# Routed experts of a mixture-of-experts layer: a flat loop over pairs of row blocks, two buffers per stage of a block, and lookup tables in block order

## The chip, the core and the metric

The kernel runs on one core of one Trainium2 chip. The metric is the device time of one execution in microseconds (us), lower is better. TensorE is called PE in the profile, VectorE DVE, ScalarE ACT, GpSimd POOL and SyncE SP; PEld is the part of PE that loads the stationary operand.

## What is computed

One decoder layer over 1024 tokens of width 1024, in float32: a token mixer (gated delta rule and a convolution branch), a normalisation, a mixture of experts with 64 experts, and a normalisation. The change touches the experts:

```python
eidx, wts = route(xf, w_router, router_bias)      # 8 of 64 experts for each of 1024 tokens
# the 8192 (token, expert) pairs, sorted by expert, in blocks of 128 rows; each block has one expert
def expert_block(args):
    xblk, e = args
    hid = jax.nn.silu(xblk @ w_gate[e]) * (xblk @ w_up[e])     # 1024 -> 256
    return hid @ w_down[e]                                     # 256 -> 1024
y = segment_sum(yb * row_w[:, None], row_tok)                  # weighted sum over a token's 8 rows
```

An expert's weights are 3 MB (gate and up 1 MB each, down 1 MB), 192 MB for all 64. A block whose expert has fewer rows is padded.

## The kernel before

Every fp32 matmul operand is split in two fp32r parts (`hi`, rounded by ACT, and `lo`, the rest, by DVE), and a product is three matmuls (`split3`, lines 58 to 60). The stage `experts` (from line 1983) works expert by expert; an expert owns one to eight blocks. Which engine does what:

- SP loads the weights in six pieces of 512 KB an expert into six raw buffers `e_raw`, each when DVE has finished with that buffer (L2050 to L2058).
- ACT rounds a piece (`e_hi`, `ed_hi`, L2193), DVE subtracts (`e_lo`, `ed_lo`, L2250). The pieces of expert e+2 are split during the first block of expert e; there are three sets of split weights.
- POOL gathers a block's 128 token rows by an indirect DMA into a landing buffer `x_landing` (L2076), copies them to `x_gather` (L2084) once PE has transposed the rows before, and scatters the finished rows `y_block` four blocks later (L2096, `LAG` = 4). Landing buffer, `x_gather`, `gu_ps`, `hidden` and `y_block` exist once.
- PE does for a block: 24 matmuls gate|up, with the 8 transposes of the next block's rows after the 18th (L2130); 12 matmuls `down` of the previous block; 2 transposes of this block's `hidden` (L2153), which wait for ACT's silu (L2207) and DVE's product (L2260).
- ACT and DVE handle, in program order, the split pieces 0 to 3, the activation, the split of the next block's rows (`xg_hi` L2196, `xg_lo` L2255), the copy of y (L2201, before the split of `hid` on ACT), the split of `hid` (L2214, L2265), then pieces 4 and 5.

The loop over experts is unrolled by three (`all_experts`, L2038), so that PE's operand addresses are constants. For each expert every engine loads two numbers from the table `plan` into registers, the number of its blocks and the number of its first one (L2030, L2031), and loops over the blocks.

The stage before it, `block_tables` (L1948), turns the 64 x 8 x 128 slots of the routing (expert, block, row) into three tables with one column for each of the 512 possible blocks: token, weight and output row. Here 64 experts have 93 blocks. In this text a "single" is an expert with one block.

Of the kernel before, what the change touches and what calls it, by code (L numbers as in the profile page):

```python
# [16 lines left out]
F32 = mybir.dt.float32  # L17
# [29 lines left out]
MAXB = S * TOPK // P + E  # L47

# [20 lines left out]
class Kernel:  # L69
# [50 lines left out]
    def constants(self):  # L120
# [21 lines left out]
        self.credit_d = nc.dram_tensor("credit", (2, P, 1), F32, kind="Internal").ap()  # L142
# [19 lines left out]
    def load_x(self):  # L162
        nc, a = self.nc, self.a
        with ExitStack() as ctx:
# [59 lines left out]
            def _(pool):  # L224
# [15 lines left out]
                link(g.memset(junk[:], NONE))  # L240
                g.memset(junk[:, :, 1:2], 0.0).then_inc(fill_ready, 2)
# [1399 lines left out]
    def shared_and_route(self):  # L1641
# [3 lines left out]
        with ExitStack() as ctx:  # L1645
# [34 lines left out]
            nb = sb(ctx, "n_blocks", [P, E])  # L1680
            nbc = sb(ctx, "n_blocks_cum", [P, E])
# [123 lines left out]
            def _(dve):  # L1805
# [102 lines left out]
                step(v.tensor_copy(self.plan[:, :, 0:1], nb[0:1, :].unsqueeze(2)))  # L1908
                step(v.tensor_copy(self.plan[:, :, 1:2], nbc[0:1, :].unsqueeze(2)))
# [10 lines left out]
            def _(pool):  # L1920
# [27 lines left out]
    def block_tables(self):  # L1948
# [3 lines left out]
        with ExitStack() as ctx:  # L1952
            rows = sb(ctx, "slot_rows", [P, Q, P, 3])
            ps = ctx.enter_context(nc.psum_tensor("tab_ps", [P, 3, Q, P], F32))
            r_in, tr_done, tab = self.sems(ctx, "rows_in", "tab_tr", "tab_done")
            cols = [sb(ctx, f"tab_col{i}", [P, Q, P]) for i in range(3)]
            block = ctx.enter_context(nc.Block())
# [17 lines left out]
            def _(pe):
                for i in range(3):
                    pe.wait_ge(tab, i + 1)
                    for q in range(Q):
                        last = nc.tensor.transpose(ps[:, i, q, :], cols[i][:, q, :], self.ident[:])
                    last.then_inc(tr_done, 1)  # L1980


    def experts(self):

        nc, sb, a = self.nc, self.sb, self.a
        with ExitStack() as ctx:
            PIECES = 6
            BUFS = 3
            SLOTS = 6
            LAG = 4  # L1990
            raw = [sb(ctx, f"e_raw{q}", [P, 4 * FF]) for q in range(SLOTS)]
            wh = [sb(ctx, f"e_hi{j}", [P, KT, 2, FF], F32R) for j in range(BUFS)]
            wl = [sb(ctx, f"e_lo{j}", [P, KT, 2, FF], F32R) for j in range(BUFS)]
            dh = [sb(ctx, f"ed_hi{j}", [P, 2, D], F32R) for j in range(BUFS)]
            dl = [sb(ctx, f"ed_lo{j}", [P, 2, D], F32R) for j in range(BUFS)]
            xl_d = sb(ctx, "x_landing", [P, D])
            xg = sb(ctx, "x_gather", [P, D])
            xh = sb(ctx, "xg_hi", [P, KT, P], F32R)
            xl = sb(ctx, "xg_lo", [P, KT, P], F32R)
            sg = sb(ctx, "gate_act", [P, FF])  # L2000
            hid = sb(ctx, "hidden", [P, FF])
            hh = sb(ctx, "hid_hi", [P, 2, P], F32R)
            hl = sb(ctx, "hid_lo", [P, 2, P], F32R)
            yb = sb(ctx, "y_block", [P, D])

            idx_g, idx_s = (sb(ctx, n, [P, 1], U32) for n in ("idx_gather", "idx_scatter"))
# [453 lines left out]
```

## Time and profile before

| | us |
|---|---|
| median of 3 timed runs (2982.14 to 2989.01) | 2988.53 |
| the profiled execution, its own time | 2998.25 |
| its span, first to last instruction | 2996.7 |
| PE busy (86%) | 2573.5 |
| DVE busy (62%) | 1864.5 |
| ACT busy (42%) | 1264.2 |
| POOL busy (26%) | 766.6 |

Times below are us from the start of the span. The expert stage starts at 1835.7 us with the first load of weights and ends at about 2865 us with the last scatter. Matmuls overlap in the profile: one of 512 columns is drawn as 0.39 us long while the next starts 0.23 us after it. PE's idle time and the distance between starts therefore say more than its busy sum. The granted clock (PEclk) is a share of full speed.

### The profile page before, as it was taken

What the parts mean: (1) busy time and instruction counts of PE and PEld (TensorE: products, weight loads), DVE (VectorE), ACT (ScalarE), POOL (GpSimd) and SP (SyncE); (2) the same over time, 40 slices, a digit from 0 to 9 for tenths busy, and PEclk for the clock granted to TensorE, in tenths of its full rate; (3) what the DMA queues carried; (4) which work ended last, traced back from release to release, by engine and by line L of the source; (5) the groups of instructions that cost most, each with busy time, mean ns of one, the idle gap of its engine ahead of it and who ended that gap; (6) DMA issues with size and microseconds to landing.
All of it is one profiled execution on the core that took longest, in us unless ns stands there. A gap on an engine that the chain in (4) does not pass through costs nothing. (4 is left out here: it accounts for less than half of the span.)

```text
span 2996.7 us, 39317 instructions
## 1 busy us (share of the span) xinstructions
PE 2573.5 (86%) x12548; PEld 2072.5 (69%) x12549; DVE 1864.5 (62%) x2441; ACT 1264.2 (42%) x1673; POOL 766.6 (26%) x888
## 2 busy tenths in 40 slices
PE   7989998998999999969977832899999989998956
PEld 5768777777877777747856721677777767776832
DVE  3346887787788655527446613676677676667428
ACT  3343453354345333335221102566566675566400
POOL 2012111222211111100002072444444444444300
PEclk9999999999999999989989965999999999999978
DMA  5423345342322353263543135788778787879367
GB/s 117 67 44 63 64 47 53 64 57 50 78 54 47 71 78 78 61 207 123 170 149 105 60 72 171 249 282 274 256 279 284 268 304 261 263 262 331 129 268 320
DMA packets 246349, 462.96 MB, mean 154 GB/s; under 512 B 26649, under 2 KB 151065, under 8 KB 244191
## 3 DMA queue, kind: packets, MB, share of 16 engines
q1 hardware_dynamic: 211870, 377.44, 45.1%
q0 software_dynamic: 34368, 84.04, 8.0%
q8 instruction: 72, 1.18, 0.2%
q14 instruction: 39, 0.31, 0.0%
HBM read 399.97 MB, written 93.87 MB: 165 GB/s over the span
## 5 line engine op out<-in xcount | busy, mean ns | idle before, releaser
L58 PE MATMUL dn_pj<-x_hi,dn_hi 128*128 128x512 f32 x1024 | 437.7, 427 | 5.1 <-DVE dn_lo L924 2.9
L60 PE MATMUL dn_pj<-x_hi,dn_lo 128*128 128x512 f32 x1024 | 411.0, 401 | 0.0
L59 PE MATMUL dn_pj<-x_lo,dn_hi 128*128 128x512 f32 x1024 | 409.8, 400 | 0.0
L1008 DVE SCALAR_TENSOR_TENSOR uc_half<-u_in,par,uc_half 128x512 f32<-128x512 f32 x480 | 383.3, 798 | 13.1
L2250 DVE TENSOR_TENSOR e_lo<-e_raw,e_hi 128x1024 fp32r<-128x1024 f32 x256 | 340.4, 1389 | 74.1 <-ACT e_hi L2193 68.0
L58 PE MATMUL gu_ps<-e_hi,xg_hi 128*128 128x512 f32 x744 | 317.8, 427 | 56.2 <-DVE xg_lo L2255 32.0
L2193 ACT ACTIVATE e_hi<-e_raw 128x1024 fp32r<-128x1024 f32 x256 | 251.9, 1052 | 141.6 <-DMA e_raw<-in_w_gate_e_dram 116.5
L60 PE MATMUL gu_ps<-e_hi,xg_lo 128*128 128x512 f32 x744 | 300.2, 403 | 0.0
L59 PE MATMUL gu_ps<-e_lo,xg_hi 128*128 128x512 f32 x744 | 300.0, 403 | 0.0
L1147 POOL TENSOR_TENSOR a_lvl<-a_t,lvl_mask 128x512 f32<-128x512 f32 x112 | 167.7, 1514 | 349.0 <-PE dn_a L686 221.1
L60 PEld LDWEIGHTS dn_pj<-x_hi,dn_lo 128*128 128x128 f32 x1024 | 198.5, 194 | 45.8
L58 PEld LDWEIGHTS dn_pj<-x_hi,dn_hi 128*128 128x128 f32 x1024 | 200.8, 196 | 39.3 <-DVE dn_lo L924 3.3
L59 PEld LDWEIGHTS dn_pj<-x_lo,dn_hi 128*128 128x128 f32 x1024 | 199.9, 195 | 34.7 <-issue 1.0
L58 PEld LDWEIGHTS gu_ps<-e_hi,xg_hi 128*128 128x128 f32 x744 | 145.6, 196 | 98.8 <-issue 68.0
L2084 POOL COPY x_gather<-x_landing 128x1024 f32<-128x1024 f32 x93 | 130.8, 1407 | 255.2 <-PE xg_ps L2130 191.7
L869 ACT ACTIVATE y_sb<-dn_a 128x256 f32<-128x256 f32 x96 | 36.8, 383 | 345.9 <-PE dn_a L686 345.5
L2250 DVE TENSOR_TENSOR ed_lo<-e_raw,ed_hi 128x1024 fp32r<-128x1024 f32 x128 | 153.4, 1239 | 31.9 <-ACT ed_hi L2193 24.2
L60 PEld LDWEIGHTS gu_ps<-e_hi,xg_lo 128*128 128x128 f32 x744 | 145.1, 195 | 33.2
L59 PEld LDWEIGHTS gu_ps<-e_lo,xg_hi 128*128 128x128 f32 x744 | 145.7, 196 | 25.3
L2201 ACT ACTIVATE y_block<-y_ps 128x1024 f32<-128x1024 f32 x93 | 95.3, 1025 | 150.4 <-PE y_ps L60 116.8
L58 PE MATMUL y_ps<-ed_hi,hid_hi 128*128 128x512 f32 x372 | 145.0, 390 | 2.4 <-DVE hid_lo L2265 2.4
L924 DVE TENSOR_TENSOR dn_lo<-dn_raw,dn_hi 128x1024 fp32r<-128x1024 f32 x62 | 92.8, 1498 | 86.6 <-ACT dn_hi L758 85.6
(346 smaller groups left out, 5183.1 us busy)
## 6 DMA issues: line engine op xcount, KB each, us to landing
e_raw<-in_w_gate_e_dram SPq DMA_DIRECT2D x128, 512.0 KB
e_raw<-in_w_up_e_dram SPq DMA_DIRECT2D x128, 512.0 KB
e_raw<-in_w_down_e_dram SPq DMA_DIRECT2D x128, 512.0 KB
dn_raw<-in_w_in_dram SPq DMA_DIRECT2D x64, 512.0 KB
y_rows<-y_rows SPq DMA_DIRECT2D x8, 2560.0 KB, 30.7
y_rows<-y_rows SPq DMA_DIRECT2D x8, 1536.0 KB, 25.1
gate_rows<-qkv_next SPq DMA_DIRECT2D x16, 512.0 KB, 3.1
br_raw<-in_w_oa_dram SPq DMA_DIRECT2D x16, 512.0 KB
```

Source lines behind the costliest of these rows:

```text
L58: nc.tensor.matmul(out, w_hi, x_hi, start=first, stop=False)
L59: nc.tensor.matmul(out, w_hi, x_lo, start=False, stop=False)
L60: return nc.tensor.matmul(out, w_lo, x_hi, start=False, stop=last)
L869: A(yy[:], ga[:, :, 0:P // 2], ACT.Copy).then_inc(y_evac, 1)
L924: tt(r["lo"][j][:], r["raw"][j][:], r["hi"][j][:].bitcast(F32), ALU.subtract).then_inc(r["w_ready"], 1)
L1008: ins = stt(out=uc[:], in0=u_in[:, t:t + HALF], scalar=w, in1=uc[:], op0=ALU.mult, op1=ALU.add)
L1147: tt(atl[l % NA][:], at[:], self.lvl_mask[:, l, :].unsqueeze(1).to_broadcast([P, 4, P]), ALU.mult).then_inc(masked, 1)
L2084: g.tensor_copy(xg[:], xl_d[:]).then_inc(x_here, 1)
L2193: A(h, r, ACT.Copy).then_inc(hi_s, 1)
L2201: A(yb[:], fl(yp[:]), ACT.Copy).then_inc(y_ready, 1)
L2250: tt(l, r, h.bitcast(F32), ALU.subtract).then_inc(lo_s, 1)
```

## The change

1. PE and POOL no longer loop over experts but over pairs of blocks (blocks 0 and 1, 2 and 3, ...), so that the buffer of a block is known by its parity. The number of blocks is rounded up to an even one, by a block without rows of the last expert. PE reads each block's expert from a table; its weight operands get their address from registers. ACT and DVE keep their loop over experts.
2. `x_gather`, `gu_ps`, `ht_ps`, `hidden` and its splits, and `y_block` have two buffers; the landing buffer and its copy are gone, the gather writes `x_gather` directly. The gather of a block is issued once PE has transposed the rows two blocks before it.
3. PE's order within a block is new: the 8 transposes of the next block come first, then 12 gate|up matmuls, the 2 transposes of the previous block's `hidden`, 12 gate|up matmuls, and the previous block's 12 `down` matmuls.
4. ACT and DVE take the split of the next block's rows and of `hid` first, and the weights in three pieces of 1 MB (two of gate|up, one of down) in three raw buffers. Gate|up are split two experts ahead, down in the first block of its own expert; split down weights have two sets.
5. `block_tables` makes tables in block order, of 128 columns: DVE works out which block each slot column belongs to, builds a 0/1 matrix `sel` and PE multiplies by it, where before it transposed.

```diff
-            raw = [sb(ctx, f"e_raw{q}", [P, 4 * FF]) for q in range(SLOTS)]
+            raw = [sb(ctx, f"e_raw{i}", [P, 2, 4 * FF]) for i in range(GU + 1)]
-                    pool.wait_ge(xg_in, n * 16 + 16)
-                    pool.wait_ge(t_done, n * 2 + 2)
-                    g.tensor_copy(xg[:], xl_d[:]).then_inc(x_here, 1)
+                    pool.wait_ge(idx_c, n + 1)
+                    pool.wait_ge(t_done, n * 2 + 2)
+                    pool.indirect_dma_start(xg[s][:], None, self.x1_d, bass.IndirectOffsetOnAxis(idx_g[s][:, 0:1], 0),
+                                            bounds_check=S - 1, oob_is_err=False).then_inc(xg_in[s], 16)
...
+                def blk(n, m, s, e, e_prev):
+                    pe.wait_ge(xl_s, n * 2 + 2)
+                    pe.wait_ge(xg_in[1 - s], (m + s) * 16 + 32)
+                    transposes(1 - s)
+                    pe.wait_ge(lo_s, e * GU + 1)
+                    gate_up(e, s, range(0, 4))
+                    if e_prev is not None:
+                        pe.wait_ge(hid_s, n)
+                        hid_t(1 - s)
+                    pe.wait_ge(lo_s, e * GU + 2)
+                    gate_up(e, s, range(4, 8)).then_inc(gu_done, 1)
+                    if e_prev is not None:
+                        pe.wait_ge(hl_s, n)
+                        pe.wait_ge(dlo_s, e_prev + 1)
+                        pe.wait_ge(y_ready, n + LAG - 1)
+                        down(e_prev, 1 - s)
...
+                with pe.Fori(1, half) as m:
+                    e_prev, e = expert_of(m * 2 - 1), expert_of(m * 2)
+                    e_next = expert_of(m * 2 + 1)
+                    blk(m * 2, m, 0, e, e_prev)
+                    blk(m * 2 + 1, m, 1, e_next, e)
...
+                    x_lo(n + 1, 0)
+                    x_lo(n + 1, 1)
+                    if not first or not known or e > 0:
+                        hid_lo(n - 1)
+                    if first:
+                        lo(e, GU)
+                    product(n)
+                    if ahead:
+                        lo(e + 2, 0)
+                        lo(e + 2, 1)
```

PE's program at the change of an expert, before: the transposes of `hidden`, then the loads of two numbers for the next expert (`TENSOR_LOAD plan`) with their register work, then the first gate|up matmul.

```order
L2153 MATMUL ht_ps<-ident,hidden 128x128
L2176 REGISTER_ALU
L2176 COMPARE_AND_BRANCH
L2175 UNCONDITIONAL_BRANCH
L2038 UNCONDITIONAL_BRANCH
L2038 ISA
L2030 TENSOR_LOAD plan
L2030 ISA x2
L2031 ISA
L2031 TENSOR_LOAD plan
L2031 ISA x2
L58 MATMUL gu_ps<-e_hi,xg_hi 128x512
```

The same engine now, at the start of the loop over pairs: three numbers are loaded for two blocks, behind the last `down` matmul of the pair before, and each group of three matmuls has two register instructions.

```order
L2257 TENSOR_LOAD block_expert
L2257 ISA x3
L2257 TENSOR_LOAD block_expert
L2257 ISA x2
L2232 MATMUL xg_ps<-ident,x_gather 128x128 x7
L59 MATMUL gu_ps<-e_hi,xg_hi 128x512
L60 REGISTER_ALU
L60 MATMUL gu_ps<-e_lo,xg_hi 128x512
L61 MATMUL gu_ps<-e_hi,xg_lo 128x512
L59 ISA
```

So the loads have left the place behind `hidden`, and register work has come between the matmuls. DVE's program in the first block of an expert, before (`hidden` stands behind four `e_lo`):

```order
L2250 TENSOR_TENSOR e_lo<-e_raw,e_hi 128x4x256
L2259 REGISTER_ALU
L2260 SCALAR_TENSOR_TENSOR hidden<-gate_act,wt_tab,gu_ps 128x256
L2253 ISA
L2255 TENSOR_TENSOR xg_lo<-xg_ps,xg_hi 128x512
L2265 TENSOR_TENSOR hid_lo<-ht_ps,hid_hi 128x256
```

and now:

```order
L2372 TENSOR_TENSOR xg_lo<-xg_ps,xg_hi 128x512
L2376 ISA
L2376 TENSOR_TENSOR hid_lo<-ht_ps,hid_hi 128x256
L2366 TENSOR_TENSOR ed_lo<-e_raw,ed_hi 128x2048
L2381 ISA x2
L2381 SCALAR_TENSOR_TENSOR hidden<-hidden,wt_tab,gu_ps 128x256
L2363 TENSOR_TENSOR e_lo<-e_raw,e_hi 128x2x4x256
```

`hidden` now stands ahead of both gate|up pieces and behind one down piece, and the next block's rows stand first.

## Rows read from the trace of the kernel before

**Rows 1.** Windows: start:end, length, busy us per engine (instructions), PEclk, DMA share, GB/s.
```profile
1825.50:1835.70 10.20, 2.82 (x12) 2.42 (x12) 3.40 (x6) 0.00 (x0) 0.00 (x0) 0.59 0.26 79
1835.70:1859.70 24.00, 1.97 (x8) 1.57 (x8) 7.97 (x8) 7.58 (x9) 9.81 (x14) 0.53 0.89 271
1859.70:1913.30 53.60, 40.44 (x172) 31.96 (x172) 36.18 (x38) 30.20 (x40) 24.76 (x31) 0.85 0.66 229
1913.30:2800.40 887.10, 816.71 (x3819) 662.51 (x3818) 616.60 (x681) 554.82 (x762) 375.78 (x496) 0.98 0.81 275
2410.20:2482.70 72.50, 62.27 (x276) 49.76 (x276) 57.55 (x60) 49.36 (x66) 27.44 (x36) 0.93 0.92 326
2494.00:2542.40 48.40, 47.59 (x230) 39.15 (x230) 28.79 (x35) 25.91 (x39) 19.78 (x30) 1.00 0.73 246
2900.00:2950.00 50.00, 39.85 (x74) 16.66 (x75) 34.55 (x40) 1.18 (x4) 0.00 (x0) 0.83 1.01 425
```

**Rows 2.** Timeline of PE: start, length, first gate|up matmul of five blocks, idle before.
```profile
2322.70 0.49 PE L58 MATMUL gu_ps<-e_hi,xg_hi 128*128 128x512 f32 x1
2332.06 0.50 PE L58 MATMUL gu_ps<-e_hi,xg_hi 128*128 128x512 f32 x1
...
2410.23 0.49 PE L58 MATMUL gu_ps<-e_hi,xg_hi 128*128 128x512 f32 x1 [1.18 <-DVE xg_lo L2255]
...
2482.72 0.49 PE L58 MATMUL gu_ps<-e_hi,xg_hi 128*128 128x512 f32 x1 [0.16 <-issue]
...
2553.58 0.49 PE L58 MATMUL gu_ps<-e_hi,xg_hi 128*128 128x512 f32 x1 [1.54 <-issue]
```

**Rows 3.** Waits, 1880 to 2840 us: who waited for whom, total, times, longest.
```profile
POOL x_gather L2084 <- PE xg_ps L2130: 191.7, 66, 8.3
...
ACT y_block L2201 <- DMA y_rows<-y_block,idx_scatter: 32.2, 12, 7.6
...
PE gu_ps L58 <- DVE xg_lo L2255: 30.5, 27, 1.6
...
PE gu_ps L58 <- issue: 22.8, 28, 2.0
PE ht_ps L2153 <- DVE hidden L2260: 22.5, 22, 6.3
...
ACT e_hi L2193 <- DMA e_raw<-in_w_up_e_dram: 6.9, 7, 2.2
```

**Rows 4.** PE and its sequencer at a change of expert: timeline, then the loads (ns min/median/max).
```profile
2302.36 0.49 PE L58 MATMUL gu_ps<-e_hi,xg_hi 128*128 128x512 f32 x1 [0.81 <-issue]
...
L2030 PEldq TENSOR_LOAD <-plan x65: 297/306/672, 1856.4 to 2855.6; - x65
```

**Rows 5.** Groups by line, 1800 to 2900 us: xcount | busy us, mean ns | idle before.
```profile
L2250 DVE TENSOR_TENSOR e_lo<-e_raw,e_hi 128x1024 fp32r<-128x1024 f32 x256 | 340.4, 1389 | 74.1 <-ACT e_hi L2193 68.0 <-issue 6.0
...
L2250 DVE TENSOR_TENSOR ed_lo<-e_raw,ed_hi 128x1024 fp32r<-128x1024 f32 x128 | 153.4, 1239 | 31.9 <-ACT ed_hi L2193 24.2 <-issue 7.7
...
L2084 POOL COPY x_gather<-x_landing 128x1024 f32<-128x1024 f32 x93 | 130.8, 1407 | 255.2 <-PE xg_ps L2130 191.7 <-DMA x_landing<-x_table,idx_gather 63.5
...
L2255 DVE TENSOR_TENSOR xg_lo<-xg_ps,xg_hi 128x512 fp32r<-128x512 f32 x188 | 120.2, 680 | 3.7 <-ACT xg_hi L2196 3.7
...
L2260 DVE SCALAR_TENSOR_TENSOR hidden<-gate_act,wt_tab,gu_ps 128x256 f32<-128x256 f32 x93 | 44.1, 474 | 111.3 <-ACT gate_act L2207 106.9 <-issue 4.4
L2265 DVE TENSOR_TENSOR hid_lo<-ht_ps,hid_hi 128x256 fp32r<-128x256 f32 x93 | 39.3, 422 | 118.8 <-ACT hid_hi L2214 111.9 <-issue 6.4
```

**Rows 6.** Timeline of the tables and of the start of the experts.
```profile
1832.78 0.69 DVE L1972 COPY wt_tab<-tab_ps 128x512 f32<-128x512 f32 x1 [0.16 <-PE tab_ps L1979]
...
1849.21 0.18 POOL L2092 COPY idx_scatter<-late_rows 128x1 uint32 x1 [6.19 <-DMA credit<-ong]
...
1855.27 1.03 POOL L2084 COPY x_gather<-x_landing 128x1024 f32<-128x1024 f32 x1 [2.89 <-DMA x_landing<-x_table,idx_gather]
...
1874.22 0.69 PE L2153 MATMUL ht_ps<-ident,hidden 128*128 128x128 f32 x2 [5.54 <-DVE hidden L2260]
```

More of the change, by code:

```diff
@@ L47 @@
 MAXB = S * TOPK // P + E
+LAG = 4
 COL_QKVZ, COL_AB, COL_GLU, COL_GA = 0, 4 * D, 4 * D + 2 * H, 6 * D + 2 * H
@@ new lines, in _ @@
+                tt(before[:], twice[:], ends[:, E - 1:E].to_broadcast([P, E]), ALU.is_lt)
+                step(v.tensor_scalar(gone[:], ends[:], part_no[:], None, ALU.is_le))
+                v.tensor_reduce(half[:], before[:], AX.X, ALU.add)
+                step(v.tensor_reduce(e_col[:], gone[:], AX.X, ALU.add))
+                v.tensor_scalar(e_col[:], e_col[:], float(E - 1), None, ALU.min).then_inc(tab, 1)
+                step(v.scalar_tensor_tensor(out=odd[:], in0=half[:], scalar=2.0, in1=base[:, E - 1:E], op0=ALU.mult,
+                                            op1=ALU.subtract))
@@ L1986, in experts @@
         with ExitStack() as ctx:
-            PIECES = 6
+            GU = 2
             BUFS = 3
-            SLOTS = 6
-            LAG = 4
-            raw = [sb(ctx, f"e_raw{q}", [P, 4 * FF]) for q in range(SLOTS)]
[L1992 to L2006, printed above, removed]
@@ L2007, in experts @@
-            late_rows = sb(ctx, "late_rows", [P, MAXB + NT + LAG], U32)
-            gu = ctx.enter_context(nc.psum_tensor("gu_ps", [P, 2, FF], F32))
+            raw = [sb(ctx, f"e_raw{i}", [P, 2, 4 * FF]) for i in range(GU + 1)]
+            wh = sb(ctx, "e_hi", [P, BUFS, KT, 2, FF], F32R)
+            wl = sb(ctx, "e_lo", [P, BUFS, KT, 2, FF], F32R)
+            dh = sb(ctx, "ed_hi", [P, 2, 2, D], F32R)
+            dl = sb(ctx, "ed_lo", [P, 2, 2, D], F32R)
+            xg = [sb(ctx, f"x_gather{s}", [P, D]) for s in range(2)]
@@ new lines, in experts @@
+            xh = sb(ctx, "xg_hi", [P, 2, KT, P], F32R)
+            xl = sb(ctx, "xg_lo", [P, 2, KT, P], F32R)
+            hid = sb(ctx, "hidden", [P, 2, FF])
+            hh = sb(ctx, "hid_hi", [P, 2, 2, P], F32R)
+            hl = sb(ctx, "hid_lo", [P, 2, 2, P], F32R)
+            yb = sb(ctx, "y_block", [P, 2, D])
+            idx_g = [sb(ctx, f"idx_gather{s}", [P, 1], U32) for s in range(2)]
+            idx_s = [sb(ctx, f"idx_scatter{s}", [P, 1], U32) for s in range(2)]
+            gu = ctx.enter_context(nc.psum_tensor("gu_ps", [P, 2, 2, FF], F32))
@@ L2114, in _ @@
-                total = pool.value_load(self.plan[0:1, E - 1, 1:2], min_val=0, max_val=MAXB - 1) + \
-                    pool.value_load(self.plan[0:1, E - 1, 0:1], min_val=1, max_val=NT)
+                half = pairs(pool)
+                with pool.Fori(0, half) as m:
+                    for s in range(2):
+                        n = m * 2 + s
+                        gather_rows(n, m, s)
+                        scatter_rows(n, s)
+                        gather(n, s)
+                        scatter(n, s)
@@ L2241, in _ @@
+                for i in range(GU):
+                    hi(0, i)
+                x_hi(0, 0)
+                x_hi(0, 1)
+                for i in range(GU):
+                    hi(1, i)
+                all_experts(act, blk)
+                total = pairs(act) * 2
+                hid_hi(total - 1)
+                y_move(total - 1)
             @block.vector
@@ L2282, in _ @@
+                for i in range(GU):
+                    lo(0, i)
                 x_lo(0, 0)
                 x_lo(0, 1)
-                for i in range(PIECES):
-                    lo(1, 1, i)
-                all_experts(dve, expert)
+                for i in range(GU):
+                    lo(1, i)
+                all_experts(dve, blk)
+                total = pairs(dve) * 2
+                hid_lo(total - 1)
     def final_norm(self):
```

447 lines of the change are left out of this document (252 added, 195 removed).

## The prediction

> **What bounds the kernel now.** I read the windows first, then block starts on PE, waits, and groups. The change lives in the expert stage, so everything before 1825.5 us and after the last scatter stays. From 1913.3 to 2800.4 us PE does 83 of the 93 blocks in 887.1 us, 10.7 us each, and DMA is busy 0.81 at 275 GB/s [rows 1]. A block in which PE waits for nothing takes 9.36 us (2322.70 to 2332.06) [rows 2]. So PE sets the pace, with 1.3 us a block lost. Where? The starts of the 83 blocks (the timeline's first is 1913.3, its last 2800.4) fall into kinds: 10 first blocks of a longer expert that follow a longer one take 9.4 us on average, 25 second or later blocks 9.9, 14 first blocks of a longer expert behind a single 10.5, 14 singles behind a longer expert 11.4 (one of them: 2542.4 to 2553.58, [rows 2]), and 20 singles behind a single 11.9. The stretch 2410.23 to 2482.72 is six such singles at 12.1 each [rows 2]; its DMA share is 0.92 at 326 GB/s. The stretch 2494.0 to 2542.4 is five blocks at 9.7, with 0.73 at 246 GB/s [rows 1].
>
> Two things hold a single back. First, order: DVE does four `e_lo` before `hidden`, then the rows of the next block, and PE waits at `ht_ps` for `hidden` (22.5 us in all), and at `gu_ps` for `xg_lo` (30.5) and for its own sequencer (22.8) [rows 3]. The last is the two table loads of a new expert, 0.3 us each plus register work; they stand behind the transposes of `hidden`, so when those have waited nothing hides them: gaps of 0.81 and 1.54 us [rows 2, 4]. ACT waits for weights hardly at all (6.9 us for the largest) [rows 3], so DMA is near its limit in runs of singles but not the one that ends last. Second, that limit: 326 GB/s over 72.5 us and six blocks is 3.94 MB a single; at share 1 the same traffic would run at 326/0.92 = 354 GB/s, 11.1 us a single. That is what a faster PE runs into.
>
> The Trainium skill bears on this: "HBM Reference" (Specifications) gives about 358 GB/s as the effective share of a core. By that figure alone a single would take 3.94/358 = 11.0 us, and the run of singles could gain no more than 1 us a block; it speaks against a large gain. The same page (Specifications) says that a core streaming alone reaches about 425 GB/s. This trace shows 425 in the last stage, from 2900 us, but in other traffic [rows 1].
>
> **The change, part by part.**
>
> *The waits at hidden, xg_lo and the copy.* PE's wait for `hidden` now stands behind down (12 x 0.23 = 2.7 us), 8 transposes and 12 gate|up matmuls, over 6 us after the gate|up sums it comes from; before it was 2.7 us. The next block's rows are transposed at the start of a block and needed one block later. DVE puts `hidden` ahead of the gate|up pieces. So 30.5 + 22.5 us go, where DVE keeps up. Its work for a single is now 4 x 1.22 (`e_lo`) + 2 x 1.24 (`ed_lo`) + 2 x 0.68 + 0.47 + 0.42 = 9.6 us [rows 5], 9.4 if large pieces save a little; I take 1.22 for `e_lo`, as its twin `ed_lo` has, since its mean of 1.39 comes beside POOL's copy (1.4 us x 93), which is gone. That is as long as PE's 9.36, so in a run of singles DVE is late, too, but by less than DMA. The Trainium skill, "GPSIMD Engine Reference" (Key points), says that GpSimd shares its SBUF interfaces with VectorE for instructions with two SBUF inputs, which `e_lo` is. By that, all of the 0.17 us x 256 = 44 us of DVE time is given back; it lies off PE's path except in runs of singles.
>
> *The copy and the landing buffer.* POOL waited 191.7 us for PE there [rows 3], which cost nothing: PE never waited for `x_gather` in steady state. Removed at 0. The new gather of a block is issued two blocks ahead of its use, some 19 us, so it is covered; without cover a landing would show as 3 to 12 us in front of the transposes.
>
> *Second y_block.* ACT waited 32.2 us for scatters, up to 7.6 at once [rows 3]; that falls to 0, and counts at the start below.
>
> *Sequencer.* Three loads for two blocks. One load is 0.31 us [rows 4]; where two stood uncovered the gap was 1.54 us [rows 2], so a load with its register work is about 0.77 us, and three with the loop's own steps are 2.6 us a pair. They stand behind the 12 `down` matmuls, whose wait (`hid_lo`) is met early, so 2.7 us of queued matmuls cover them. Bounds: 0 and 2.6 us a pair; I take 0.3, 0.15 us a block, near the lower end, because the wait ahead of the cover is early. The 24 register instructions that address the weights in a block are unlike anything PE did: the nearest are those around the loads: (1.54 - 2 x 0.31) us for the eight `ISA` of the order before, 0.12 us each. Two take 0.24 of the 0.68 us that three matmuls last, so I take 0; if they don't fit, rival C.
>
> Together: 9.36 + 0.15 = 9.5 us for 63 blocks (all but singles behind singles) = 598.5 us. An isolated single is late by at most 2 us in DMA and DVE, and the new slack of several us takes it.
>
> *Runs of singles, 20 blocks.* Bounds: 11.1 (DMA at share 1) and 12.5 (now 12.1 in the long run, plus 0.4 for coarser pieces: three 1 MB buffers wait for two 2.4 us steps each before they are refilled, where six smaller ones refilled sooner). Middle of 11.1 and 12.1: 11.6, so 232 us. After each of the 7 runs DVE and DMA catch up: 1.5 us each, 10.5 us (bounds 0 and 3). Sum 841 against 887.1: **-46 us**.
>
> *The start.* The gather of block 0 now waits for the credit DMA, which landed at 1849.21; before it went out as soon as the stage had begun (1835.7), its rows were copied at 1855.27 [rows 6], and the first gate|up came at 1859.7, 4.4 us behind. Now the issue comes after 1849.2, 13.5 us into the stage, and the second gather must land, too, before PE starts. If the landing takes as little as 3 us (an estimate: no row shows it alone), PE starts earlier than before; if it takes what was left of 19.6 us, 10 us later. I take 5 us later (bounds -1 and 10). Blocks 0 to 3 took 53.6 us [rows 1] with waits of 5.54 [rows 6] and 6.3 us [rows 3] for `hidden`, behind pieces and a late scatter; I take 9 back of these 11.8. Together **-4**.
>
> *An extra block.* 93 is odd, so PE does 94: **+9.4** (it moves no rows, but PE runs it whole).
>
> *The tables.* The stage took 10.2 us [rows 1], of which DVE waited for rows. New are some 21 small DVE operations, at 0.2 us for small ones and up to 0.69 us for 512 elements [rows 6], 7 us in all, of which 5 lie in the wait for the rows, less 1.4 us for narrower copies out of PSUM, and PE's products as the transposes before: **+3** (bounds 0 and 8).
>
> Sum: -46 - 4 + 9.4 + 3 = -37.6 us. The profiled execution of 2998.25 us is 9.7 above the median of 2988.53; I carry the difference over: 2951 us.
>
> **The rivals.**
>
> A (0.55), the forecast: runs of singles stay at DMA's limit, the rest goes at PE's pace.
>
> B (0.15), DMA isn't the limit. Share 0.92 in the run is queueing, and the 425 GB/s of [rows 1] can be had: 3.94 MB take 9.3 us. Then the 20 blocks take 9.6 and the catching up goes: -40 - 10.5 more, about 2900 us. For it: ACT hardly waits for DMA now. Against: 326 GB/s is the most that any stretch of weights and rows shows. The page on HBM named above holds both figures, and doesn't decide.
>
> C (0.18), slower: register instructions between the matmuls. PE's sequencer has two more per three matmuls. The point from which it decides: if a group's dispatch takes longer than 0.68 us. Each 0.1 us over costs 12 x 94 x 0.1 = 113 us, so 2951 + 113 = 3064 us; 0.04 us over is enough to be slower than before. For it: table loads do show as gaps at PE. Against: 0.24 us of 0.68, by the steps at the loads.
>
> D (0.12), no change that can be told (within 0.3%, 9 us, which is about what a measurement of this kernel can tell). Three raw buffers of 1 MB refill too late: a load waits for the end of a 2.1 us and a 2.4 us step of its own buffer, down is only one expert ahead, and each single, isolated or not, takes 12.1. Then 34 blocks take 12.1 = 411, 49 take 9.5 = 466: 877, and -10 - 4 + 9.4 + 3 = -2: 2987 us. For it: less is loaded ahead (7 MB instead of 9). Against: in one expert's time all three buffers still have a load in flight nearly always.
>
> **How the numbers follow.** Faster: A + B = 0.70. Same: D = 0.12. Slower: C = 0.18. The range goes from B's 2900, of which I leave some out, to beyond D: 2903 to 2996. A alone reaches from 20 x 0.5 + 10.5 lower (DMA at share 1, nothing to catch up) to 20 x 0.9 + 10.5 + 5 higher (12.5 us, catching up 3 us, a late start): 2931 to 2985.
>
> **What would show it.** In the trace after: PE's waits for `hidden` and `xg_lo` below 5 us together; blocks of longer experts at 9.4 to 9.6 us; in runs of singles 11.1 to 12.1 us, with a DMA share over 0.95 and ACT or DVE now waiting for `e_raw`; 94 blocks; gaps at the start of each pair below 0.5 us; `e_lo` at 2.4 us for 2048 elements; the first gate|up 42 us after the tables' stage began, against 34.2 before (1825.5 to 1859.7). If matmuls within a block start over 0.23 us apart, C is right; if the runs go at 9.5, B. The prediction fails, too, if the sequencer's loads aren't hidden behind down: 2.3 us more in each of 47 pairs is 108 us, and the gain is gone.

## The result, and the profile after

The changed kernel takes 3002.36 us (median; 2996.38 to 3007.55), the kernel before 2988.77 us in the same series: a ratio of 1.0044, 95% interval 1.0029 to 1.006. It is slower by about 14 us, 0.4%. The forecast was 2951 us, 1.3% faster, with a range of 2903 to 2996: wrong in sign, and outside the range.

The profiled execution took 3002.1 us, with a span of 3000.5. First the windows of the changed kernel, cut at the same events as [rows 1]: tables, start of the experts, blocks 0 to 3, blocks 4 to 86, a run of six one-block experts, and a stretch of longer experts.

```profile
1814.00:1826.90 12.90, 5.25 (x25) 4.79 (x25) 7.31 (x29) 0.00 (x0) 2.10 (x11) 0.58 0.21 62
1826.90:1856.80 29.90, 3.62 (x17) 3.22 (x17) 6.56 (x5) 7.44 (x6) 14.03 (x18) 0.52 0.66 195
1856.80:1899.80 43.00, 38.75 (x173) 31.23 (x171) 26.90 (x24) 24.24 (x26) 13.72 (x16) 0.90 0.70 249
1899.80:2793.80 894.00, 813.46 (x3820) 659.72 (x3820) 562.61 (x508) 541.68 (x590) 272.81 (x332) 0.97 0.78 272
2411.00:2485.20 74.20, 61.37 (x278) 48.52 (x278) 54.44 (x44) 48.78 (x48) 21.17 (x24) 0.95 0.91 323
2495.30:2543.00 47.70, 47.40 (x233) 38.92 (x232) 27.15 (x28) 29.55 (x35) 14.87 (x20) 1.00 0.63 221
```

Against [rows 1]: from the tables' first load to PE's first gate|up 42.8 us, before 34.2 (+8.6). Blocks 0 to 3 43.0, before 53.6 (-10.6). The 83 blocks 894.0, before 887.1 (+6.9, where the prediction had -46). From block 87 to the last stage's first transfer 84.4, before 74.7 (+9.7, the extra block). The last stage is longer by 0.7. That is +15.3 us. In the profile of before the stages ahead of the tables ended 11.6 us later than here (1825.7 against 1814.1); the change doesn't touch them. In all later profiles, one of a variant of the kernel before among them, this mark stands at 1808 to 1818, so it moves from one execution to another, and I leave it out. The medians differ by 13.6 us, near the sum of 15.3.

PE's stretch of longer experts runs as forecast: five blocks in 47.7 us, 9.54 each. The run of six one-block experts takes 74.2 us, before 72.5 [rows 1]. The waits of the changed kernel, 1880 to 2840 us, say who is late:

```profile
POOL y_rows L2200 <- ACT y_block L2322: 488.0, 69, 13.7
...
ACT e_hi L2303 <- DMA e_raw<-in_w_up_e_dram: 124.6, 70, 4.2
...
PE y_ps L59 <- DVE hid_lo L2376: 63.6, 30, 4.5
...
ACT y_block L2322 <- DMA y_rows<-y_block,idx_scatter: 38.3, 11, 6.4
...
PE xg_ps L2232 <- issue: 17.5, 23, 1.0
```

PE's waits for `xg_lo` (30.5 us in [rows 3]) and for `hidden` (22.5) are gone. In their place stands one at the down product, 63.6 us, for `hid_lo`. And ACT, which waited 6.9 us for weights [rows 3], now waits 124.6. The timeline of the changed kernel shows how the second makes the first (start, length, engine, operation, idle before and releaser):

```profile
2704.59 1.92 ACT L2303 ACTIVATE e_hi<-e_raw 128x2048 f32 x1 [2.48 <-DMA e_raw<-in_w_up_e_dram]
...
2705.32 0.33 SPq L2153 DMA_DIRECT2D e_raw<-in_w_gate_e_dram  x1
...
2706.68 2.29 DVE L2363 TENSOR_TENSOR e_lo<-e_raw,e_hi 128x2048 f32 x1 [1.52 <-ACT e_hi L2303]
...
2709.09 1.29 DVE L2372 TENSOR_TENSOR xg_lo<-xg_ps,xg_hi 128x512 f32 x2
2709.13 0.33 SPq L2153 DMA_DIRECT2D e_raw<-in_w_gate_e_dram  x1
2709.56 0.38 SPq L2153 DMA_DIRECT2D e_raw<-in_w_up_e_dram  x1
...
2710.29 0.41 DVE L2376 TENSOR_TENSOR hid_lo<-ht_ps,hid_hi  x1
...
2711.13 0.79 PE L59 MATMUL y_ps<-ed_hi,hid_hi 128*128 x1 [4.50 <-DVE hid_lo L2376]
...
2715.77 1.91 ACT L2303 ACTIVATE e_hi<-e_raw 128x2048 f32 x1 [2.90 <-DMA e_raw<-in_w_up_e_dram]
...
2717.59 1.01 ACT L2322 ACTIVATE y_block<-y_ps 128x1024 f32 x1
...
2717.85 2.29 DVE L2363 TENSOR_TENSOR e_lo<-e_raw,e_hi 128x2048 f32 x1 [1.94 <-ACT e_hi L2303]
...
2718.50 1.08 ACT L2309 ACTIVATE xg_hi<-xg_ps 128x512 f32 x2
...
2720.30 0.33 SPq L2153 DMA_DIRECT2D e_raw<-in_w_gate_e_dram  x1
```

Follow one raw buffer. DVE's low part ends at 2708.97; at 2709.13 SP asks for the next 1 MB into it (two transfers of 512 KB); at 2715.77 ACT can take it (6.6 us, in which ACT stood idle 2.90); ACT 1.91, DVE 2.29; at 2720.30 SP may ask again. This turn of the loop is 11.2 us long, and no step of it waited for PE.

How PE gets to wait is seen one turn earlier. ACT stood idle 2.48 us for the same buffer and began its `e_hi` at 2704.59; so DVE's `e_lo` began 1.52 us late, at 2706.68. ACT and DVE work in order: on ACT `y_block`, the next rows' `xg_hi` and `hid_hi` stand behind the `e_hi` that waited, on DVE `xg_lo` and then `hid_lo` (2710.29) behind the `e_lo`. PE comes to down after 12 matmuls and finds `hid_lo` 4.50 us late. The wait costs twice. The windows behind it (columns as above) show the granted clock at the lower level, 1.2 GHz, for most of the 12 matmuls of down (nine take 0.63 us instead of 0.39), and at 2.4 GHz again in the next block:

```profile
2711.10:2715.60 4.50, 4.47 (x11) 3.55 (x12) 4.26 (x3) 1.77 (x2) 2.80 (x1) 0.50 0.93 307
2716.90:2722.60 5.70, 5.70 (x28) 4.69 (x28) 3.91 (x4) 4.49 (x6) 2.26 (x4) 1.00 0.91 339
```

For the comparison of kernels I cut blocks 4 to 86 at each first gate|up matmul, and sort the 83 stretches by whether DVE splits a new expert's weights in them (between two activations). 25 are without weights; the others stand alone, or first, in the middle (20) or last in a row of such stretches. The expectations below call the 20 "singles behind singles" and the last ones "first blocks behind a single". In the kernel before the block named is the one whose gate|up opens the stretch; in the changed kernel, whose activations come later, the one before it. Means in us, worked out from the timelines; each row is one profiled execution, so a few us in the last column tell nothing:

| kernel | no weights | alone | first | middle | last | blocks 4 to 86 |
|---|---|---|---|---|---|---|
| before | 9.92 | 9.42 | 11.38 | 11.92 | 10.52 | 887.1 |
| after | 9.48 | 9.90 | 9.87 | 12.51 | 11.97 | 894.0 |
| e1_fine | 9.48 | 10.04 | 10.06 | 10.83 | 10.90 | 848.3 |
| e2_light | 9.48 | 9.90 | 9.87 | 10.50 | 10.47 | 831.1 |
| e3_early_hid | 9.31 | 9.32 | 10.55 | 12.08 | 11.07 | 872.2 |
| e4_before_coarse | 10.36 | 9.53 | 11.51 | 12.76 | 10.93 | 923.5 |
| e5_fine_early | 9.36 | 9.31 | 9.47 | 10.71 | 10.66 | 824.6 |
| e6_finer | 9.49 | 10.69 | 10.71 | 11.03 | 10.53 | 861.8 |
| e7_fine_copy | 9.50 | 10.33 | 10.16 | 11.35 | 10.89 | 862.9 |
| e8_fine_early_light | 9.31 | 9.33 | 9.42 | 9.41 | 9.54 | 779.9 |

### The profile page after: what moved, and what is told of

It is laid out like the page before. It is cut to its first block and busy times, and to the rows that moved or that the text cites. A ratio compares the mean times of both kernels' runs of the same rounds, so it can differ in the third digit from the quotient of the medians.

```text
span 3000.5 us, 42077 instructions
## 1 busy us (share of the span) xinstructions
PE 2580.1 (86%) x12607; PEld 2079.5 (69%) x12608; DVE 1809.9 (60%) x2274; ACT 1250.2 (42%) x1486; POOL 657.2 (22%) x718
## 5 line engine op out<-in xcount | busy, mean ns | idle before, releaser
L2303 ACT ACTIVATE e_hi<-e_raw 128x2048 f32 (+1 forms) x128 | 244.7, 1913 | 244.2 <-DMA e_raw<-in_w_up_e_dram 244.2
L2363 DVE TENSOR_TENSOR e_lo<-e_raw,e_hi 128x2048 f32 (+1 forms) x128 | 290.4, 2287 | 51.5 <-ACT e_hi L2303 51.2
L59 PE MATMUL gu_ps<-e_hi,xg_hi 128*128 (+1 forms) x752 | 310.4, 413 | 0.0
L2200 POOL DMA_INDIRECT y_rows<-y_block,idx_scatter x98 | 160.5, 1637 | 626.0 <-ACT y_block L2322 514.0
L61 PE MATMUL gu_ps<-e_hi,xg_lo 128*128 (+1 forms) x752 | 294.3, 391 | 0.0
L60 PE MATMUL gu_ps<-e_lo,xg_hi 128*128 (+1 forms) x752 | 293.5, 390 | 0.0
L2372 DVE TENSOR_TENSOR xg_lo<-xg_ps,xg_hi 128x512 f32 (+1 forms) x190 | 122.1, 684 | 168.4 <-ACT xg_hi L2309 154.9
L59 PE MATMUL y_ps<-ed_hi,hid_hi 128*128 (+1 forms) x376 | 160.4, 426 | 69.4 <-DVE hid_lo L2376 68.8
L2366 DVE TENSOR_TENSOR ed_lo<-e_raw,ed_hi 128x2048 f32 (+1 forms) x64 | 146.8, 2293 | 59.8 <-ACT ed_hi L2303 58.5
L61 PE MATMUL y_ps<-ed_hi,hid_lo 128*128 (+1 forms) x376 | 156.1, 415 | 0.0
```

The costliest lines, as they stand in the source:

```text
L59: nc.tensor.matmul(out, w_hi, x_hi, start=first, stop=False)
L60: nc.tensor.matmul(out, w_hi, x_lo, start=False, stop=False)
L61: return nc.tensor.matmul(out, w_lo, x_hi, start=False, stop=last)
L2200: pool.indirect_dma_start(self.yr_d, bass.IndirectOffsetOnAxis(idx_s[s][:, 0:1], 0), yb[:, s, :], None, bounds_check=S * TOPK - 1, oob_is_ ...
L2303: A(h, r, ACT.Copy).then_inc(hi_s if i < GU else dhi_s, 1)
L2363: tt(l, r, h.bitcast(F32), ALU.subtract).then_inc(lo_s, 1)
```

## The experiments

### e1_fine: the changed kernel in pieces of 512 KB

Six raw buffers instead of three of twice the size, with the same bytes in all and the same order on every engine. A transfer has 512 KB in both kernels; what differs is the buffer that is held, and the steps of ACT and DVE that hold it.

```diff
-            GU = 2
-            raw = [sb(ctx, f"e_raw{i}", [P, 2, 4 * FF]) for i in range(GU + 1)]
+            GU = 4
+            raw = [sb(ctx, f"e_raw{i}", [P, 4 * FF]) for i in range(GU + 2)]
...
-                    pe.wait_ge(lo_s, e * GU + 1)
+                    pe.wait_ge(lo_s, e * GU + 2)
```

> The changed kernel with six raw buffers and pieces of 512 KB again, in the same order (down's two, gate|up's first two, the activation, gate|up's last two). Three theories for the steady stretch, blocks 4 to 86, which now takes 894 us with 12.5 us for a single behind a single. R (refill): a 1 MB buffer is refilled only after a 1.9 us and a 2.3 us step, so ACT waits for weights (124.6 us against 6.9) and everything behind it on ACT with it. Expects the stretch at 865 to 878 us, singles behind singles at 11.5 to 12.0, ACT's waits for weights below 60 us, the ratio to before at 0.995 to 1.000. Q (queue and cover): the split of the hidden rows has only 12 matmuls, 2.7 us, of cover on PE and stands behind a weight piece on ACT, whatever its size. Expects 888 to 897 us, PE still waiting over 50 us at down. L (limit): DMA carries no more than 323 to 326 GB/s in such runs. Expects no change, 890 to 897 us.

Measured: 2962.01 us, ratio to before 0.9911 (0.989 to 0.9933). This edit turns the change from 0.4% slower to 0.9% faster: 40 us by the ratios, 46 in the 83 blocks of the profiled executions. It changes the size of a buffer together with their number; more buffers of 1 MB were not tried, so which of the two counts is open. The waits and windows of this kernel (83 blocks, then the six of the run):

```profile
ACT e_hi L2303 <- DMA e_raw<-in_w_up_e_dram: 65.7, 65, 2.1
...
PE xg_ps L2232 <- issue: 27.8, 33, 1.4
PE y_ps L59 <- DVE hid_lo L2379: 26.3, 26, 1.9
```

```profile
1895.70:2744.00 848.30, 796.65 (x3819) 643.47 (x3819) 571.64 (x681) 563.40 (x765) 222.05 (x332) 1.00 0.83 288
2385.70:2450.40 64.70, 58.15 (x279) 46.34 (x278) 54.91 (x63) 52.04 (x68) 16.52 (x24) 1.00 0.99 369
```

Three things are seen here. PE's wait for `hid_lo` falls from 63.6 to 26.3 us, its longest from 4.5 to 1.9; the clock is granted in full over all 83 blocks (0.97 before this edit); and DMA works 0.99 of the run at 369 GB/s, where the coarse pieces left it idle in 0.09 of it, at 323. The 10.83 us of a middle stretch are below the 11.1 that the prediction had as a floor. Q and L of the expectations are refuted. R has the direction and the cause, but the gain is larger than it said (848.3 us against 865 to 878), while ACT still waits 65.7 us, where it had less than 60.

Of the 46 us, 29 are idle time of PE that goes (80.5 us before the edit, 51.7 now), and 17 are busy time (813.46 less 796.65): the same matmuls at a granted clock of 1.00 instead of 0.97.

### e3_early_hid: the hidden rows' transposes first

1 MB pieces as in the change; the two transposes of `hidden` stand ahead of the 24 gate|up matmuls of the next block, so `hid_lo` has all 24 as cover instead of 12.

```diff
                     transposes(1 - s)
-                    pe.wait_ge(lo_s, e * GU + 1)
-                    gate_up(e, s, range(0, 4))
                     if e_prev is not None:
                         pe.wait_ge(hid_s, n)
                         hid_t(1 - s)
+                    pe.wait_ge(lo_s, e * GU + 1)
+                    gate_up(e, s, range(0, 4))
```

> The changed kernel with PE's two transposes of the previous block's hidden rows moved ahead of all 24 gate|up matmuls (behind the transposes of the next block's rows), so that their split has 5.4 us of cover instead of 2.7. Q: PE's wait at down falls from 63.6 us to below 20, singles behind singles to 11.6 or less, the stretch to 865 to 875 us. R and L: the wait at down falls only partly or turns up elsewhere (at the hidden rows' transposes, or at the weights), the stretch stays within 5 us of 894.

Measured: 2977.83 us, 0.9962 (0.9948 to 0.9976); blocks 4 to 86 872.2 us, 21.8 less than after. Waits:

```profile
ACT e_hi L2303 <- DMA e_raw<-in_w_up_e_dram: 123.0, 70, 3.3
...
PE y_ps L59 <- DVE hid_lo L2376: 37.2, 31, 3.0
...
PE ht_ps L2245 <- DVE hidden L2381: 24.8, 23, 1.8
```

ACT waits for weights about as long as in the changed kernel (123.0 us, there 124.6), so the refill is as late as it was. PE's wait at down falls from 63.6 to 37.2, but 24.8 come back in front of the transposes, and its waits for its own sequencer fall from 17.5 only to 13.0. The window of the 83 blocks says where the gain is:

```profile
1897.90:2770.10 872.20, 797.70 (x3821) 653.20 (x3819) 561.46 (x507) 540.78 (x591) 274.96 (x332) 1.00 0.80 279
```

PE's idle time falls by 6 us alone, from 80.5 to 74.5. The other 16 us are busy time, 813.46 less 797.70: the longest wait at down is now 3.0 us instead of 4.5, and the granted clock 1.00 instead of 0.97. Part of that is clock. Another part is the order itself: stretches without weights, in which PE hardly waits in either kernel, fall from 9.48 to 9.31 us, a difference whose cause isn't shown. At 512 KB, where the clock is 1.00 with and without this edit, it takes 7 us off the busy time (e5_fine_early below), so some 9 of the 16 us are clock, an estimate. Stretches alone fall from 9.90 to 9.32; there PE had waited 0.42 us on average for its sequencer at a pair's start, and no longer does. That the sequencer can run ahead past down once `hid_lo` comes early is the likely reason, and was not tried by itself. Neither expectation holds: 872.2 us is Q's figure, but the wait turned up elsewhere, as R and L had it, and the middle stretches (12.08) stay above Q's 11.6.

### e4_before_coarse: only the coarse pieces, in the kernel before

```diff
-            PIECES = 6
+            PIECES = 3
             BUFS = 3
-            SLOTS = 6
+            SLOTS = 3
```

> The kernel before with nothing but the piece size of the change: three raw buffers and pieces of 1 MB, in the places of the order before. R: slower, the stretch of blocks 4 to 86 at 900 to 915 us against 887.1, ratio 1.004 to 1.010, ACT's waits for weights above 60 us. Q and L: within 4 us of 887.1. This run is also a second look at the stages ahead of the experts, which ended at 1825.7 us in the one profile of before and at 1814.1 in that of the change.

Measured: 3031.17 us, 1.0154 (1.0125 to 1.0183). The middle stretches go from 11.92 to 12.76, the 83 blocks from 887.1 to 923.5, more than the 900 to 915 expected by R; ACT waits 33.4 us for the weights of up, where R had more than 60. Q and L, which expected no change, are refuted. So 1 MB pieces cost 36 us over the 83 blocks in the order of before (46 by the ratio) and 46 in the order of after (40 by the ratios), and the rest of the change, extra block included, is worth about 27 us of gain (e1_fine against before, by the ratio).

### e2_light: half of the weights' bytes

The changed kernel, but half of each piece isn't loaded and stays zero, so the output isn't the reference's; every step of every engine stays.

```diff
-    sp.dma_start(raw[i][:, n, :].rearrange("p (k f) -> p k f", k=4), src).then_inc(w_in[i], 16)
+    sp.dma_start(raw[i][:, n, :].rearrange("p (k f) -> p k f", k=4)[:, 0:2, :], src[:, 0:2, :]).then_inc(w_in[i], 16)
```

> The changed kernel with half of the bytes of each weight load left out (the raw buffers are set to zero once, so half of the weights are zero); all instructions on PE, ACT, DVE and POOL stay. R and L: both need late weights, so singles fall to 9.4 to 10.0 us and the stretch of blocks 4 to 86 to 790 to 815 us, the whole to about 2915 us. Q: the order alone costs, singles stay above 11 us and the stretch above 860 us. If register work on PE cost anything, it would be left here as blocks above 9.5 us.

Measured: 2934.5 us in one execution; 83 blocks 831.1 us, between the 790 to 815 of R and L and the 860 of Q, and the middle stretches at 10.50, between their 10.0 and 11. With half the bytes ACT still waits for them:

```profile
ACT e_hi L2304 <- DMA e_raw<-in_w_up_e_dram: 63.3, 63, 3.1
...
PE xg_ps L2233 <- issue: 25.0, 33, 1.0
...
PE y_ps L59 <- DVE hid_lo L2377: 16.7, 19, 1.9
```

A rate limit alone is unlikely to do that at a DMA share of 0.60 (183 GB/s over the 83 blocks). What the coarse loop costs beside the bytes is told by e8, below.

### e5_fine_early: both edits

> The changed kernel with both edits at once: six raw buffers of 512 KB, and the transposes of the hidden rows ahead of all gate|up matmuls. With pieces of 512 KB a single behind a single took 10.83 us at the start of its gate|up and PE lost 26.2 us to the low part of the hidden rows in 26 waits; that wait is what the early transposes give 12 matmuls more cover. If the two losses are separate (refill and short cover): the 20 singles go to 10.3 us or less, the first blocks of longer experts behind a single to 10.5 or less, first blocks from 10.0 to 9.4, blocks 4 to 86 from 848 to 825 to 835 us, and the time to 2940 to 2950 us. If the short cover was only a sign of late weights (DVE behind), the early order gives nothing on top: 2958 to 2965 us. If weights from HBM are at their limit at 10.8 us a single (3.94 MB, 364 GB/s), the singles stay at 10.8 and only the first blocks gain 0.5 us each on 23 blocks: about 2950 us, with the singles telling it apart.

Measured: 2921.44 us (2918.32 to 2928.45), 0.9797 (0.9775 to 0.9819): 2% faster than before, and 19 to 29 us under the expected time. Some 6 us of that are the series' (the kernel before took 2983.58 us in it, 2989.95 in that of e1_fine), and in the profile the stages ahead of the experts ended 7.0 us earlier than e1_fine's (1808.1 against 1815.1). The 83 blocks took 824.6 us, just below the 825 to 835 expected. The two edits add up: late transposes 894.0 and 848.3 (1 MB, 512 KB), early ones 872.2 and 824.6; the size gives 46 or 48, the order 22 or 24. By the ratios, each known within some 0.2% or 6 us, it is 40 and 49, 25 and 34. So each edit gains about the same with and without the other. What it gains is not the same time: at 512 KB, with the clock at 1.00 on both sides, the order gives 17 us of idle and 7 of busy time. Waits, then the windows of the 83 blocks and of the run of six:

```profile
ACT e_hi L2303 <- DMA e_raw<-in_w_up_e_dram: 59.6, 64, 1.8
...
ACT e_hi L2303 <- DMA e_raw<-in_w_gate_e_dram: 16.5, 28, 1.6
PE y_ps L59 <- DVE hid_lo L2379: 15.7, 20, 1.9
```

```profile
1888.50:2713.10 824.60, 789.63 (x3822) 649.41 (x3820) 570.01 (x682) 561.73 (x765) 240.34 (x332) 1.00 0.84 296
2363.70:2426.60 62.90, 58.30 (x278) 46.60 (x277) 53.34 (x61) 51.34 (x66) 15.34 (x24) 1.00 0.99 377
```

The stretches alone (9.31) and without weights (9.36) are at PE's own pace. The middle ones hardly moved (10.83 to 10.71), at a DMA share of 0.99: the part of the expectation that had them at 10.3 or less fell, the one that had weights at their limit stands.

### e8_fine_early_light: what holds the run now

The best version with half of the weights' bytes (the other halves zero, so the output isn't the reference's).

```diff
-    sp.dma_start(raw[i][:].rearrange("p (k f) -> p k f", k=4), src).then_inc(w_in[i], 16)
+    sp.dma_start(raw[i][:].rearrange("p (k f) -> p k f", k=4)[:, 0:2, :], src[:, 0:2, :]).then_inc(w_in[i], 16)
```

> The version with 512 KB pieces and the early transposes of the hidden rows, with half of the weights' bytes left out (the other halves of the raw buffers are zero, so the output isn't the reference's); all steps of ACT, DVE and PE as they are, each refilled in the same order. What holds a single behind a single at 10.71 us there, 0.95 of it as PE's idle time? If it is the rate at which weights come (3.94 MB in 10.71 us are 368 GB/s), halving the bytes brings the 20 singles to what DVE needs: 6 x 1.22 + 2 x 0.68 + 0.48 + 0.42 = 9.6 us, first blocks behind singles to 9.5, so 20 x 1.1 + 15 x 1.1 = 38 us less: 2880 to 2895 us, and ACT's waits for the weights of up near 0. If it is still the refill loop (SP, a transfer's fixed time, ACT's and DVE's step), the singles stay above 10.3 us: 2908 to 2920 us.

Measured: 2880.86 us, 0.9632 (0.9605 to 0.9658), as expected for a limit of bytes. Both windows:

```profile
1893.60:2673.50 779.90, 778.11 (x3820) 650.85 (x3819) 565.92 (x681) 551.59 (x764) 218.07 (x332) 1.00 0.63 195
2345.20:2401.70 56.50, 56.44 (x279) 46.96 (x277) 53.15 (x61) 49.22 (x66) 16.64 (x24) 1.00 0.80 244
```

PE is busy 778.1 of 779.9 us: 9.40 us a block, middle stretches 9.41. DVE's 9.6 us of work for a block with weights, which I had as the next bound, was none: it has 53.15 us to do in 56.50, 8.9 a block. (The sum of its mean durations, 9.6, counts too much, since its records overlap a little.) So in e5_fine_early the bytes of weights and rows are what is left, 45 us over the 83 blocks. With the same bytes e2_light took 831.1: the coarse loop and the late transposes cost 51 us even where bytes are few, and 69 (894.0 less 824.6) where they are all there.

### e6_finer: 256 KB pieces

```diff
-            GU = 4
+            GU = 8
-            raw = [sb(ctx, f"e_raw{i}", [P, 4 * FF]) for i in range(GU + 2)]
+            raw = [sb(ctx, f"e_raw{i}", [P, 2 * FF]) for i in range(GU + 4)]
```

> The changed kernel in pieces of 256 KB: twelve raw buffers, as many bytes of buffer as before, and each refilled as soon as its own two steps (about 0.55 us on ACT, 0.65 us on DVE) are done. Dose and response of the refill theory: singles behind singles 12.51 us at 1 MB, 10.83 at 512 KB; a piece of half the size opens its buffer about 1.1 us sooner, so 10.2 to 10.6 here, first blocks behind singles 10.5, blocks 4 to 86 about 840 us, the time 2950 to 2958 us. Against it: twice as many instructions on ACT and DVE, each with a fixed cost (from rows: 2287 ns for 2048 elements against half of it for 1024, so little), and twice the transfers for SP. If DVE becomes the bound through them, or HBM is the limit at 10.8, no gain: 2960 to 2970 us.

Measured: 2964.24 us, 0.9935 (0.9913 to 0.9956): no gain over e1_fine, and 861.8 us for the 83 blocks, 13 more. The groups of e1_fine and then of this kernel (1800 to 2900 us) tell why:

```profile
L2366 DVE TENSOR_TENSOR e_lo<-e_raw,e_hi 128x1024 f32 x244 | 282.2, 1218 | 1.1 <-ACT e_hi L2303 1.1
```

```profile
L2367 DVE TENSOR_TENSOR e_lo<-e_raw,e_hi 128x512 f32 x488 | 299.4, 685 | 1.6 <-ACT e_hi L2304 1.4
L2304 ACT ACTIVATE e_hi<-e_raw 128x512 f32 x488 | 276.2, 624 | 41.0 <-DMA e_raw<-in_w_up_e_dram 21.7 <-DMA e_raw<-in_w_gate_e_dram 17.7
```

ACT's wait for weights nearly halves again (41.0 us in all, 74.9 in e1_fine), so the refill theory's mechanism holds; but twelve steps of 0.685 us are 8.2 us against 7.3 for six of 1.22. By mean durations DVE then needs 8.2 + 1.36 + 0.48 + 0.42 = 10.5 us for a block with weights. At the start of a row of such stretches it is busy 10.34 of 10.71 us (ACT 9.57), and stretches alone go from 10.04 to 10.69: there DVE is close to being the bound. In the run of six it isn't:

```profile
2388.50:2455.30 66.80, 57.96 (x279) 46.35 (x278) 55.38 (x96) 53.51 (x100) 21.17 (x24) 1.00 1.00 351
```

DVE works 55.38 of 66.80 us, and DMA all of it, but at 351 GB/s, where the 512 KB pieces came at 369. A transfer is of 256 KB here, half of e1_fine's. Whether the smaller transfers or the longer row of steps holds the run was not told apart.

### e7_fine_copy: GpSimd's copy put back

e1_fine with one more 128x1024 copy a block on GpSimd, between spare buffers; nothing waits for it.

```diff
                         gather(n, s)
+                        g.tensor_copy(spare[:, 1], spare[:, 0])
```

> The changed kernel with 512 KB pieces, and one more 128x1024 copy a block on GpSimd, from one spare buffer to another, as the copy that the change took out, but one that nothing waits for. If GpSimd's copy slows the two-input steps of DVE that run beside it, the mean of the low parts of gate|up (128x1024) rises from about 1.14 us to 1.25 or more (1.39 in the kernel before), DVE's busy time by 20 to 40 us, and since DVE binds only in runs of singles, these go from 10.8 to 11.0 to 11.3 us: 2964 to 2972 us. If the longer steps before had another cause, the mean stays at 1.14 us and the time at 2962 us, within 3.

Measured: 2968.1 us, 0.9948 (0.993 to 0.9967); e1_fine had 2962.01 and 0.9911, so 6 us by the medians and 11 by the ratios. The groups of this kernel, 1800 to 2900 us:

```profile
L2369 DVE TENSOR_TENSOR e_lo<-e_raw,e_hi 128x1024 f32 x244 | 284.1, 1225 | 0.6 <-ACT e_hi L2306 0.6
L2372 DVE TENSOR_TENSOR ed_lo<-e_raw,ed_hi 128x1024 f32 x122 | 191.8, 1612 | 11.6 <-ACT ed_hi L2306 11.5
L2219 POOL COPY spare<-spare 128x1024 f32<-128x1024 f32 x94 | 100.9, 1073 | 0.1
```

I had expected the slower steps among `e_lo`, where they were before [rows 5]. They are among `ed_lo`, 1612 ns against 1219 in e1_fine: at its new place in GpSimd's order the copy lies beside those. Sorted by the timeline, from block 4 on, the 62 `ed_lo` that overlap a copy take 1.96 us on average, the 60 others 1.22; in the kernel before, 104 `e_lo` beside the copy take 1.63, the 132 others 1.22. So it is the instruction beside the copy that is slowed. The sum is what counts: DVE's busy time grows by 54 us over the whole span (1820.2 to 1874.4), some 0.58 us for each of the 94 copies. The Trainium skill, "GPSIMD Engine Reference" (Key points), says that GpSimd shares its SBUF interfaces with VectorE for instructions with two SBUF inputs; the trace agrees, `ed_lo` is one. `hid_lo`, which reads one input from PSUM, takes 0.42 us beside a copy or not.

## Why the prediction was wrong, step by step

**Runs of singles, 20 blocks: the step that failed.** It took 11.6 us, the middle of 11.1 and 12.1, and let the waits end behind the run with 1.5 us each. Measured: 12.51 for the 20, and 11.97 for the 15 last ones, which it had at 9.5. By its own sum the 83 blocks were to take 841; they took 894: 20 x 0.91 = 18 us from the middle ones, 15 x 2.47 less the 10.5 us of catching up = 27 from the last ones, and the other 48 took 9.67 instead of 9.5, 8 us. The term that failed is "0.4 for coarser pieces", the only one that priced what the change does to the buffers: e4_before_coarse shows 0.84 us a middle stretch in the order of before, and e1_fine 1.68 in the order of after. That the upper bound, 12.5, meets the measured 12.51 is luck: it starts from 12.1, the pace of one long run before, where the new order with 512 KB pieces gives 10.83. Below, 11.1 us was no floor: the division of 326 GB/s by a share of 0.92 assumes that rate goes with share, and e1_fine and e5_fine_early moved 369 and 377 GB/s at 0.99. The prediction's sentence on "HBM Reference" (Specifications) of the Trainium skill, about 358 GB/s as a core's share, gave 11.0 us; those two runs are above it, and the measurement decides.

That the waits end behind the run failed as well: PE lost time in the last stretches, too, where the price was 1.5 us for each of 7 runs.

**Rival D had the mechanism.** "Three raw buffers of 1 MB refill too late" is what happened, and the reason given against it, that all three have a load in flight nearly always, fails by the loop above: that buffer had one in flight for at most 6.6 of 11.2 us. I gave it 0.12. It was right in kind and short in price (2987): it gave 12.1 us to 34 blocks, the 14 behind a longer expert among them; stretches at the start of a row took 9.87, the 20 in the middle 12.51, and the 15 last ones 11.97. I should have laid out one buffer's loop: landing, ACT's step, DVE's step. With D's own 2.1 + 2.4 us of occupied buffer, and 6 us for the landing (an estimate: 1 MB at half of the prediction's 354 GB/s, two buffers in flight), the loop is 10.5 us before any order of work makes it wait, already longer than PE's 9.36.

**The waits at hidden and xg_lo.** They are gone, as forecast. But a wait that goes needs the question of what is late next. "Over 6 us" of cover for `hidden` was right and beside the point: the chain goes on through `ht_ps`, `hid_hi` and `hid_lo` to down, and for those the change left 12 matmuls, 2.7 us. e3_early_hid, which gives them 24, is 22 us faster over the 83 blocks, though only 6 of them are idle time of PE. The prediction says of this wait that it is "met early"; it was late 30 times.

**DVE in a run of singles, 9.4 to 9.6 us.** The durations were right (`e_lo` 2.29 us for 2048 elements, forecast 2.4), but DVE gets a block done in 8.9 us and is not the bound at 512 KB, by e8. At 256 KB it comes close, by e6.

**Sequencer.** Forecast 0.3 us a pair, measured 0.5 on average (mostly 0.7, up to 1.0) where the stretch before the pair has weights and 0.1 at the others. The reason for the low value, an early wait ahead of the cover, is what was wrong: the gap goes where `hid_lo` is early. It is gone in e3's and e5's stretches alone, stays at 13.0 us in all in e3, and is down to 1.1 us in e8. The 24 register instructions of a block were rightly put at 0: stretches without weights go at 9.48, in e8 at 9.31, and rival C's sign, matmuls over 0.23 us apart, isn't there.

**Rival B, no limit in DMA's rate.** Wrong as well: even in the best version, with DMA's share at 0.99, the run goes at 10.48 us a block (62.90 / 6), and halving the bytes gives 45 us.

**Start, extra block, tables.** First gate|up 42.8 us after the tables' first load (forecast 42); blocks 0 to 3 10.6 us faster (9); extra block 9.7 (9.4); tables +2.8 by the first weights' load (3). The copy's removal gave DVE 0.17 us an `e_lo`, as said; by e7 it is worth 6 to 11 us in a version where DVE is close to PE, more than the 0 taken for it.

**The clock.** The prediction had no term for it. Over the 83 blocks of the changed kernel the granted clock is 0.97, 26 us of full-speed time by the clock's records (22 in the kernel before, at 0.98), and the longest waits at down, 3 to 4.5 us, stand beside stretches at 1.2 GHz; not every such stretch has one. In e1_fine and e5_fine_early no wait at down was over 1.9 us and the clock stayed at 1.00; in e6 and e7, with single waits of 3.0 to 3.3, it is 0.99. So 17 of e1_fine's 46 us are busy time at the lower clock, as shown there.

## What to carry to other kernels

When a change alters the size of staging pieces, write the loop of one buffer in rows (issue, landing, each step that holds it, the semaphore that frees it) and compare it with the time of the work that it feeds; the same bytes in more buffers may be worth more than the reordering around them, until the steps get too short for their price (0.685 us for 512 elements on DVE, 1.22 for 1024) and the engine that splits them comes close to its limit. When a wait is moved off an engine's path, follow the same chain to its next consumer and count the cover that stands ahead of that one too. A rate measured at a DMA share below 1 is no ceiling to scale from: find a stretch at a share of 0.99, or halve the bytes. And when an edit takes idle time away, compare the engine's busy time and granted clock as well: part of the gain may stand there.

## What the runs showed of the hardware

One core pulled 377 GB/s of weights and rows over 62.9 us, at a share of 0.99 (e5_fine_early), in 256 KB pieces 351 GB/s at 1.00 (e6_finer), and with half of the weights' bytes 244 GB/s at 0.80 (e8_fine_early_light): share and rate don't go together. A 128x1024 copy on GpSimd (1.07 us) cost DVE 0.58 us in e7_fine_copy, nearly all of it in the `ed_lo` beside it, so an off-path copy isn't free. Register addresses in matmul operands, two register instructions for every three matmuls, cost PE nothing that shows (gate|up matmuls 0.39 us long, blocks 9.31 us in e8).
